# One decoder step on one core: order of logits and values in the loop over cached blocks

## The reference

```python
# cut to what matters
k_full = cache_k[page_table[:, :c * ppb]].astype(f32).reshape(DB, c, MOBA_BLOCK, H, Dh)
kmean = jnp.mean(k_full, axis=2)
gate = jnp.einsum('bthd,bjhd->bhtj', qf, kmean)
_, sel = lax.top_k(gate, n_sel)
...
parts.append((jnp.einsum('bthd,bhtkd->bhtk', qf, k_g.astype(f32)), v_g, 'bhtk,bhtkd->bthd'))
l_new = jnp.where(causal, jnp.einsum('bthd,bshd->bhts', qf, k.astype(f32)), -jnp.inf)
parts.append((l_new, v, 'bhts,bshd->bthd'))
probs = jax.nn.softmax(jnp.concatenate([lp for lp, _, _ in parts], axis=-1) * scale, axis=-1)
```

## Time and profile before

| | us |
|---|---|
| median of 3 runs (1374.7 to 1380.32) | 1379.77 |
| profiled execution | 1377.05 |
| span of its instructions | 1375.3 |
| TensorE busy in the span | 1226.5 (89%) |
| VectorE, ScalarE, GpSimd busy | 615.9, 415.7, 443.3 |

### The profile page before, as it was taken

One profiled execution on the slowest core, in us unless ns is written; L12 is line 12 of the kernel. 1 busy time (PEld: TensorE's weight loads), 2 busy tenths in 40 slices (PEclk: granted clock), 3 DMA queues, 4 the chain that ended last, 5 costly groups with the idle time before them and its releaser, 6 DMA issues. The chain is left out here.

```text
span 1375.3 us, 33314 instructions
## 1 busy us (share of the span) xinstructions
PE 1226.5 (89%) x14362; PEld 1106.8 (80%) x14362; DVE 615.9 (45%) x1060; ACT 415.7 (30%) x828; POOL 443.3 (32%) x305
## 2 busy tenths in 40 slices
PE   4999998888888888877678999998999999999995
PEld 3998996666666666555458999998999999999994
DVE  6367895434455445543544232224545544440003
ACT  5041331333233322122341222233433333341110
POOL 5243453101110111010022343453565555564430
PEclk9999999999999999998769999999999999999998
DMA  5222216897578769979632223221222222232221
GB/s 200 78 84 90 77 49 243 302 325 262 195 273 323 265 229 372 337 289 349 265 131 68 79 78 100 84 98 54 90 78 87 82 77 92 83 98 79 82 72 69
DMA packets 57252, 216.29 MB, mean 157 GB/s; under 512 B 6609, under 2 KB 6994, under 8 KB 56338
## 3 DMA queue, kind: packets, MB, share of 16 engines
q1 hardware_dynamic: 57106, 214.17, 43.9%
HBM read 207.78 MB, written 6.37 MB: 156 GB/s over the span
## 5 line engine op out<-in xcount | busy, mean ns | idle before, releaser
L642 PE MATMUL ps<-buffer_at 128*128 128x288 f32 (+2 forms) x5760 | 778.0, 298 | 11.4 <-DVE buffer_at L1905 6.4
L642 PEld LDWEIGHTS ps<-buffer_at 128*128 128x128 f32 x5760 | 773.8, 191 | 16.4 <-issue 10.5
L1444 POOL TENSOR_TENSOR buffer_at<-buffer_at 128x1024 fp32r<-128x1024 f32 (+1 forms) x118 | 331.6, 2813 | 386.9 <-ACT buffer_at L1179 386.3
L1179 ACT ACTIVATE buffer_at<-buffer_at 128x1024 fp32r<-128x1024 f32 (+1 forms) x118 | 128.9, 1095 | 293.6 <-PE ps L642 134.6
L1500 POOL TENSOR_TENSOR buffer_at<-buffer_at 128x256 f32<-128x256 f32 x45 | 39.9, 916 | 340.3 <-DVE buffer_at L1735 340.3
L1014 PE MATMUL ps<-buffer_at 128*32 128x128 f32 x2048 | 75.2, 290 | 29.1 <-ACT buffer_at L1298 26.3
L1014 PEld LDWEIGHTS ps<-buffer_at 128*32 128x32 f32 x2048 | 55.8, 115 | 43.0 <-ACT buffer_at L1298 37.6
L1415 ACT ACTIVATE buffer_at<-buffer_at 128x592 f32<-128x592 f32 x44 | 38.8, 883 | 162.1 <-DVE buffer_at L2099 158.9
L2097 DVE TENSOR_TENSOR buffer_at<-ps,buffer_at 128x512 f32<-128x512 f32 x44 | 30.4, 692 | 125.8 <-PE ps L642 125.8
L981 PE MATMUL ps<-buffer_at 128*32 128x256 f32 x1024 | 74.6, 412 | 6.1 <-DMA buffer_at<-in_kvcache 6.1
L1835 DVE TENSOR_REDUCE buffer_at<-ps 128x1 f32<-128x256 f32 (+1 forms) x68 | 27.9, 411 | 98.3 <-PE ps L981 98.2
(11 more groups left out here) (222 smaller groups left out, 1284.4 us busy)
## 6 DMA issues: line engine op xcount, KB each, us to landing
buffer_at<-in_kvcache SPq DMA_DIRECT2D x256, 512.0 KB, 5.2
buffer_at<-in_w_up SPq DMA_DIRECT2D x44, 512.0 KB, 3.4
buffer_at<-in_w_in SPq DMA_DIRECT2D x42, 512.0 KB, 3.5
buffer_at<-in_w_down SPq DMA_DIRECT2D x16, 704.0 KB, 4.1
buffer_at<-in_w_br SPq DMA_DIRECT2D x8, 512.0 KB, 3.5
buffer_at<-in_w_o SPq DMA_DIRECT2D x8, 512.0 KB, 3.5
buffer_at<-in_xin SPq DMA_DIRECT2D x4, 576.0 KB, 6.8
buffer_at<-in_xin SPq DMA_DIRECT2D x1, 2304.0 KB, 11.7
```

The costliest lines, as they stand in the source:

```text
L642: ins = e.matmul(out, lhs, rhs[:, cols], start=(start and i == 0), stop=(stop and i == 2))
L1179: e.activation(hi[:, :, :], raw, ACT.Copy).then_inc(w_hi, 1)
L1444: e.tensor_tensor(lo[:, :, :], raw, hi[:, :, :], ALU.subtract).then_inc(w_lo, 1)
```

## The change

It moves `qk_step(i + 1)` on TensorE from behind part 1 to right behind `turn_step(i)`, and `pv_step(i)` from behind part 0 to behind part 1. On ScalarE `exp_step(i + 1)` comes right behind `pt_out(i)`, and `o_out(i)` behind the unit of part 1. On VectorE `low_step(i + 1)` comes first in a step and `gate_step(i + 1)` behind part 1; `att_second` of part 3 of the step before moves ahead of part 0. In parts 1 and 3 the unit now comes ahead of the stage. `layout()` gets other numbers and lays all stages anew.

```diff
@@ layout
-            now += ((5, 2)[i % PER == 0], (12, 4)[i % PER == 0], (12, 3)[(i + 1) % PER == 0], 0)[part]
+            now += ((5, 2)[i % PER == 0] + (12, 3)[(i + 1) % PER == 0], 0, (12, 4)[i % PER == 0], 0)[part]
@@ TensorE
                 turn_step(i)
+                if i + 1 < STEPS:
+                    qk_step(i + 1)
                 chunk_stage(CHUNK_AT.get((i, 0)))
                 end_work(i, 0)
+                attention(UNIT_AT.get((i, 1)))
+                chunk_stage(CHUNK_AT.get((i, 1)))
                 pv_step(i)
-                chunk_stage(CHUNK_AT.get((i, 1)))
-                attention(UNIT_AT.get((i, 1)))
-                if i + 1 < STEPS:
-                    qk_step(i + 1)
                 chunk_stage(CHUNK_AT.get((i, 2)))
                 end_work(i, 2)
...
+                attention(UNIT_AT.get((i, 3)))
                 chunk_stage(CHUNK_AT.get((i, 3)))
-                attention(UNIT_AT.get((i, 3)))
@@ ScalarE
                 pt_out(i)
+                if i + 1 < STEPS:
+                    exp_step(i + 1)
                 attention(UNIT_AT.get((i - 1, 3)))
                 chunk_copies(CHUNK_AT.get((i, 0)))
                 end_work(i, 0)
-                o_out(i)
                 chunk_copies(CHUNK_AT.get((i, 1)))
                 attention(UNIT_AT.get((i, 1)))
-                if i + 1 < STEPS:
-                    exp_step(i + 1)
+                o_out(i)
@@ VectorE
-                att_first(UNIT_AT.get((i - 1, 3)))
-                chunk_out(CHUNK_AT.get((i, 0)))
-                att_second(UNIT_AT.get((i - 1, 3)))
-                end_work(i, 0)
-                chunk_out(CHUNK_AT.get((i, 1)))
-                att_first(UNIT_AT.get((i, 1)))
                 if i + 1 < STEPS:
                     low_step(i + 1)
+                att_second(UNIT_AT.get((i - 1, 3)))
+                chunk_out(CHUNK_AT.get((i, 0)))
+                end_work(i, 0)
+                att_first(UNIT_AT.get((i, 1)))
+                chunk_out(CHUNK_AT.get((i, 1)))
+                if i + 1 < STEPS:
+                    gate_step(i + 1)
                 att_second(UNIT_AT.get((i, 1)))
...
+                att_first(UNIT_AT.get((i, 3)))
                 chunk_out(CHUNK_AT.get((i, 3)))
-                if i + 1 < STEPS:
-                    gate_step(i + 1)
```

## The result

| | us |
|---|---|
| before, median of 4 runs (1374.70 to 1380.32) | 1377.98 |
| changed, median of 4 runs (1408.01 to 1413.73) | 1410.04 |
| ratio, 95% interval | 1.0234 [1.0204, 1.0264] |
| changed, profiled execution (span 1412.0) | 1413.73 |

The change makes the kernel 2.3% slower. 1390 was forecast, so the direction and the wide range held. The forecast size, 0.9%, was less than half of what came, and 1410 lies outside the 1381 to 1402 that the forecast itself stood for.

A forecast was written before the change was run, and what follows sets the result against it. Waits held the loop; 46.1 us go, but the ring then makes two steps at least A + F + 0.1. Stretches of +5.8, -0.7, +4.5, -2.1, +5.6 give +13.1 on 1377.05: 1390 us, range 1360 to 1418.

The forecast's parts named there:

- The waits that go: TensorE's values waiting for the copy of turned probabilities, 25.1 us, and turn waiting for the exponential, 21.0 us: both go.
- A: Time from the start of logits i+1 to the end of values i; forecast 4.95, 4.8, 3.35, 3.5, tail 3.8 us.
- F: Time from a ring slot being freed to its being filled again; taken as 9.95 us, range 9.1 to 12.1.
- Rivals 1 and 4: Rival 1: fills land best, F 9.1, 1365 us, chance 0.18; rival 4: ring hardly binds, F near 7.0, 1332, 0.02.
- rival 2: Gain and loss meet, F at 9.5 or smaller waits inside A: 1377 us, no change; chance 0.18.
- the floor: Shortest step the ring of cached blocks allows, half of A + F + 0.1; 7.5 us in steps 1 to 16.
- Rival 3: TensorE's clock falls in steps 36 to 56, A 5.9, step 8.0 us: +26, 1416 us; chance 0.14.
- Steps 48 to 56: Loop stretch forecast at 62.3 us for 64.4, with step 51 shorter and 4.9 us for a reload of x: -2.1.
- Steps 1 to 16: First loop stretch, A 4.95, 7.65 us a step: 122.4 us for 116.6, +5.8.
- Steps 17 to 35: Second loop stretch, 7.5 us a step: 142.5 us for 143.2, -0.7.
- Steps 57 to 66: Loop tail: five group-norm steps left at 46.7 us, five others 34.8 us for 29.2: +5.6.
- W: All of a loop step's work without the added waits between stages; forecast 6.7, 6.3, 4.7, 4.4 us by stretch.

The follow-up runs named there:

- the filler: Changed kernel plus four unread 128x256 matmuls between turn and next logits in steps 35 to 55 (not 46): 1407.59 us, run again 1405.4 us.
- the repeat: The changed kernel itself, unaltered, timed again beside the filler on one chip: 1411.01 us, 1.0227 of the kernel before.

## Why the prediction was off in size

- **The waits that go** (46.1 us): right, 3.0 are left.
- **The mechanism, two steps at least A + F + 0.1:** right. It binds in 7 of the steps 36 to 47 (the next logits that want the slot start as soon as its fill has landed); over these A is 4.71 and F 10.15 in the mean, with the 0.1 that is 14.96, and two steps take 15.00.
- **F, 9.95:** right to 0.1 to 0.3. Where the fill binds it is 10.25, 10.15, 10.15 and 10.08 in the four stretches up to step 56. Of the seven in steps 36 to 47 one is 13.3, a fill that was issued behind the load of the states (1024 KB); the other six have 9.6 in the mean. Rivals 1 and 4 needed an F below 9.5, and rival 2 that or a smaller A; none came.
- **A in steps 36 to 47, 3.35:** this is the step of the sum that failed, 9.1 of the 19.5 us that the stretches missed in all. It was priced at full clock, from matmuls of the earlier trace rows, with the wait of the floor spread evenly over the steps. But where the work of a step is far below the floor, the waits gather: a step that starts late frees its slot late, the step after finds its fill landed, and the one behind that waits for both. A wait of 2 to 5 us stands in nearly every second step, the clock falls, and A of just those steps, the ones that count, is 4.71. At 4.71 and 10.15 a step is 7.5 us, and 12 of them 90.0, as measured. With the filler's 3.16 the bound pairs took 13.35, the 13.4 of the forecast: at full clock the forecast of the floor was right. The Trainium skill (TensorE: Matmul & The Clock Gate, HAM oscillation) describes such a fall between bursts; the trace agrees, with 1.93 us for values that take 1.08. Rival 3, given 0.14, is this mechanism, and a clock well below 1.00 in steps 36 to 56 was named as a sign of being wrong: it was 0.87 and 0.84. The rival's bound step was to take 8.0 us, with A at 5.9 for the lower level throughout; it took 7.5, since only a part of A ran at that level. In steps 35 to 55 the filler gives back 5.6 us between medians, 4.5 and 9.6 between the profiles, with its own work in the sum; so about that much of the 32 us is shown to be the clock's. What the clock costs in the other stretches was not tested.
- **Steps 48 to 56 (-2.1, measured -0.9):** right to 1.2 us; the clock fell here too (0.84).
- **Steps 1 to 16 (+5.8, measured +10.3):** the mechanism held, but in the 8 bound steps A was 5.25 for 4.95 and F 10.25 for 9.95; 0.6 us per two steps, taken for all 16, is 4.8, about the 4.5 that were missed. The repeat has 124.4 us in this stretch, 2.5 less than the first profile.
- **Steps 17 to 35:** right to 1 us, by luck in part. Two bound steps took 15.3 us where 14.85 was taken, and step 20 alone took 18.0, 6.6 of it a wait for its fill; the other 18 steps took 6.9 in the mean, less than the 7.5 of the forecast.
- **Steps 57 to 66:** right to 1 us, in both of its parts. The five steps with the norm, 57 to 61, go from 662.98 to 709.65, 46.67 us where 46.7 had been left for them. The five empty ones, 62 to 66, go on to 743.61, 33.96 us for 34.8. These had luck in them: A was taken as 3.8 for every step, and in steps 61 to 64 it is 1.95, 3.64, 2.23 and 3.64, so the lower level was there in every second step only.
- **The first step, "bounded by one step's stages, 2 us" and left at nothing:** wrong, 5.5 us. The wait for the fill was seen; that VectorE's queue would stand behind it with all gram and attention results was written down for the loop and not applied to step 0.
- **The layout** was given no term of its own, and alone it gains some 14 us. That gain lies inside the stretches above.
- **Smaller slips of the working:** TensorE was busy for 78% of the fourth stretch, not 80; the stages of steps 48 to 56 come to 1.0 us a step by the prediction's own prices, not 1.15; and W comes out 0.1 to 0.3 too long. None of these moves a stretch of the sum by more than 1 us.

## What to carry to other kernels

When a consumer is moved ahead of the work that frees its buffer, price the path from freed to filled against the time between two uses before anything else, and release each part of a buffer at its own last use: here keys given back with the logits turned a loss of 2.3% into a gain of 2.7%. A floor that is longer than the work does not idle evenly; look at whether its waits gather, and price the work behind a gathered wait at the clock that the trace shows there. Where a change has two parts, a sum that holds only their joint effect hides a good part behind a bad one.

## What the runs showed of the hardware that was not expected

- Four matmuls of 128x256, put into each of 20 steps, shortened the kernel by 5.6 us between the medians, since the rest ran at the higher clock.
- DMAs of half the size, twice as many of them, landed hardly sooner. In the DMA issues of the changed kernel and then of the one with split fills (count, size, median us from issue to landing):

```profile
buffer_at<-in_kvcache SPq DMA_DIRECT2D x256, 512.0 KB, 5.0
```

```profile
buffer_at<-in_kvcache SPq DMA_DIRECT2D x512, 256.0 KB, 4.7
```

- With half as many pages of the full size, in the kernel that loads one sequence of a pair, they landed sooner:

```profile
buffer_at<-in_kvcache SPq DMA_DIRECT2D x128, 512.0 KB, 4.2
```

- In these rows the time to land goes with how much is asked for at a time more than with the size of one DMA. The gain of the split came from when the halves were asked for, not from faster transfers.
